# One layer of a hybrid decoder on Trainium2: a sixth place for expert weights, where x lies

## The reference

```python
def _back(x, mods, o_attn, o_conv, gate_a, gate_b, w_pa, w_pb, w_o, g_ffn, ...):
    gate1, shift2, scale2, gate2 = mods
    merged = jax.nn.sigmoid(gate_a) * (o_attn @ w_pa) + jax.nn.sigmoid(gate_b) * (o_conv @ w_pb)
    x = x + gate1 * (merged @ w_o)
    h = _rmsnorm(x, g_ffn) * (1 + scale2) + shift2
    return x + gate2 * _hier_moe(h, w_rg, b_rg, w_re, b_re, w_gate_e, w_up_e, w_down_e)

    # _hier_moe: a row has a weight (combine) for two of the 32 experts, 0 for the others
    a = jnp.einsum('btd,edf->btef', h, w_gate_e)      # w_gate_e, w_up_e: (32, 1024, 256)
    b = jnp.einsum('btd,edf->btef', h, w_up_e)
    return jnp.einsum('btef,efd->btd', jax.nn.silu(a) * b * combine[..., None], w_down_e)  # (32, 256, 1024)
```

## Time and profile before

| | |
|---|---|
| median of 3 runs | 839.25 us (838.13 to 840.46) |
| profiled execution, its own time | 842.34 us |
| its span | 840.6 us |
| TensorE matmuls busy | 711.9 us (85%) |
| VectorE busy | 316.9 us (38%) |
| ScalarE busy | 166.9 us (20%) |
| GpSimd busy | 121.8 us (14%) |
| moved by DMA | 194.72 MB, mean 232 GB/s |
| granted TensorE clock, mean | 0.93 |

### The profile page before, as it was taken

The page is one execution under the profiler, slowest core; times in us unless marked ns, Lnnn a source line. Parts: engine busy times, 40 slices in busy tenths (PEclk is TensorE's granted clock), DMA queues, the critical chain, the costliest instruction groups (busy, mean ns, idle before and its releaser), DMA issues.

```text
span 840.6 us, 12119 instructions
## 1 busy us (share of the span) xinstructions
PE 711.9 (85%) x5001; PEld 543.9 (65%) x5001; DVE 316.9 (38%) x691; ACT 166.9 (20%) x323; POOL 121.8 (14%) x186
## 2 busy tenths in 40 slices
PE   0799999999997799899997999789997888787810
PEld 0389898889997789899993455465554555454500
DVE  0362322136778433323223654435332121212145
ACT  0362222111441432121210111111111010101011
POOL 1500003010040000100000000123333222222011
PEclk9999999999999799999999999769999899999875
DMA  9744466863335036421208910529999999999643
GB/s 296 320 156 172 156 267 234 320 224 111 103 116 175 27 126 275 143 67 51 75 1 309 418 59 25 225 97 379 415 417 414 418 415 419 414 419 415 251 188 154
DMA packets 37439, 194.72 MB, mean 232 GB/s; under 512 B 7106, under 2 KB 7290, under 8 KB 20984
## 3 DMA queue, kind: packets, MB, share of 16 engines
q1 hardware_dynamic: 28512, 171.26, 52.0%
q0 software_dynamic: 8352, 21.81, 7.3%
q10 hardware_dynamic: 520, 0.87, 0.4%
HBM read 186.91 MB, written 15.27 MB: 241 GB/s over the span
## 4 chain that ended last, share of the span: by engine, by line
PE 77%; DVE 8%; DMA 5%; issue 5%; ACT 2%; SPq 1%; POOL 0%; POOLq 0%; DVEq 0%; ACTq 0%
PE bank L1510 29%; PE bank L1744 16%; PE bank L1763 7%; PE bank L1706 6%; PE bank L1654 3%; DMA arena_b<-in_w_ada 3%; PE bank L1449 2%; PE bank L1733 2%; PE bank L1651 2%; PE bank L1546 1%; DMA arena<-in_w_in 1%; PE bank L1671 1%; PE bank L1609 1%; PE bank L1699 1%; ACT arena_b L934 1%
## 5 line engine op out<-in xcount | busy, mean ns | idle before, releaser
L1510 PE MATMUL bank<-h_parts,w_parts 128*128 128x260 f32 x2160 | 276.5, 288 | 1.1 <-DVE w_parts L991 0.9
L1510 PEld LDWEIGHTS bank<-h_parts,w_parts 128*128 128x128 f32 x2160 | 267.1, 192 | 10.1 <-issue 8.7
L1744 PE MATMUL bank<-arena,arena_b 128*64 128x256 f32 x832 | 107.2, 415 | 21.6 <-issue 19.3
L1744 PEld LDWEIGHTS bank<-arena,arena_b 128*64 128x64 f32 x832 | 70.0, 149 | 51.4 <-issue 25.0
L991 DVE TENSOR_TENSOR w_parts<-arena,w_parts 128x1024 fp32r<-128x1024 f32 x46 | 56.3, 1223 | 66.8 <-ACT w_parts L837 66.6
L1340 DVE TENSOR_TENSOR arena_b<-bank,arena_b 128x128 f32<-128x128 f32 x32 | 9.3, 292 | 140.4 <-ACT arena_b L940 140.3
L780 POOL DMA_INDIRECT y_scratch<-arena_b x32 | 33.4, 1044 | 176.5 <-DVE arena_b L1361 161.8
L1706 PE MATMUL bank<-arena,arena_b 128*128 128x512 f32 x128 | 58.6, 612 | 0.0
L837 ACT ACTIVATE w_parts<-arena 128x1024 fp32r<-128x1024 f32 x46 | 48.5, 1054 | 43.2 <-DMA arena<-in_w_in 28.8
L1763 PE MATMUL bank<-arena,arena_b 128*64 128x512 f32 x208 | 49.5, 593 | 0.8 <-DVE arena_b L1346 0.8
L1706 PEld LDWEIGHTS bank<-arena,arena_b 128*128 128x128 f32 x128 | 24.3, 195 | 28.8 <-issue 28.7
(11 more groups left out here) (285 smaller groups left out, 769.8 us busy)
## 6 DMA issues: line engine op xcount, KB each, us to landing
arena<-in_w_gate_up SPq DMA_DIRECT2D x52, 1024.0 KB
arena<-in_w_down SPq DMA_DIRECT2D x26, 1024.0 KB
arena<-in_w_in SPq DMA_DIRECT2D x46, 512.0 KB, 5.1
arena<-in_w_ada SPq DMA_DIRECT2D x22, 1024.0 KB, 7.2
arena_b<-in_w_gate_up SPq DMA_DIRECT2D x12, 1024.0 KB
arena_b<-in_w_down SPq DMA_DIRECT2D x12, 512.0 KB
arena_b<-in_x_prompt SPq DMA_DIRECT2D x8, 512.0 KB, 13.3
arena<-in_w_o SPq DMA_DIRECT2D x2, 2048.0 KB, 8.2
```

What stands on the lines that cost most here:

```text
L1510: ins = pe.matmul(ps[s][:, 0:HALF], w_parts[:, n % 2, wp, k], h_parts[:, hp, k, s * HALF:(s + 1) * HALF], start=(k == 0 and hp == 1), stop ...
L1744: ins = pe.matmul(ps[2 + b][R * hh:R * hh + R, 0:2 * P], hTe[:, b, c * P + jj * R:c * P + jj * R + R], w_gu[slot][jj][:, c, :, hh * P:(hh ...
```

## The change

There is a sixth place. Its gate and up weights are the first 4 x 1024 columns of `X`, half of its down weights the fifth 1024 columns of `X`, and the other half the place of `h2T`. Since x lies there, SP writes each tile of x to a new tensor `x_scratch` in DRAM (`keep_x`) after the tile's two halves are summed: four tiles behind the second issue for expert 4, the last behind expert 3's loads. Expert 5 is loaded into the sixth place when the five writes have landed (`s_xw`), ScalarE has squared all of x (`s_sq2` 10) and the router has read the last of h2T (`s_rt` 5). The loop now starts at expert 6, and an expert e lies in place e mod 6. The last expert in the sixth place is 29; when its down matmuls are done (`s_y` 30) SP reads x back, and VectorE waits for all five tiles (`s_xl`) before it adds the experts' sum. Three semaphores that nothing used are gone; no other instruction of the other engines is added or removed, but the places that their matmuls read change from expert 5 on.

```diff
-SLOTS = 5
+SLOTS = 6
...
         gu_at.append([spare(0, 2 * D), spare(4 * D, 2 * D)])
+        gu_at.append([region("X", 0, 2 * D), region("X", 2 * D, 2 * D)])
...
         dn_at.append([spare(2 * D, D), spare(6 * D, D)])
+        dn_at.append([region("X", 4 * D, D), region("SPLIT", 22 * D, D)])
...
+        x_d = nc.dram_tensor("x_scratch", [T, D], F32).ap()
...
             sp.wait_ge(s_h2, 2)
             load_gate_up(4, 4, 1)
             load_down(4, 4, 1)
+
+            def keep_x(n):
+
+                i = RB[n]
+                sp.wait_ge(s_x2, 2 * n + 2)
+                sp.dma_start(x_d[i * P:i * P + rows[i]], x[0:rows[i], i]).then_inc(s_xw, 16)
+
+            for n in range(4):
+                keep_x(n)
             sp.wait_ge(s_wom, 10)
             for half in range(2):
                 load_gate_up(3, 3, half)
             load_down(3, 3, 0)
+            keep_x(4)
             sp.wait_ge(s_h2, 10)
             load_gate_up(4, 4, 0)
             load_down(4, 4, 0)
+            sp.wait_ge(s_xw, 16 * 5)
+            sp.wait_ge(s_sq2, 10)
+            sp.wait_ge(s_rt, 5)
+            for half in range(2):
+                load_gate_up(5, 5, half)
+                load_down(5, 5, half)
             for e in range(SLOTS, NE):
                 sp.wait_ge(s_gu, e - SLOTS + 1)
...
+            sp.wait_ge(s_y, NE - 2)
+            for i in range(5):
+                sp.dma_start(x[0:rows[i], i], x_d[i * P:i * P + rows[i]]).then_inc(s_xl, 16)
             sp.wait_ge(s_over, 1)
...
+            dve.wait_ge(s_xl, 16 * 5)
             summed(0)
```

More of the change, by code:

```diff
@@ L336, in hybrid_step @@
         s_modT = sem("s_modT")
-        s_modc = sem("s_modc")
         s_mod = sem("s_mod")
@@ L392, in hybrid_step @@
         s_mrg = sem("s_mrg")
-        s_a2 = sem("s_a2")
         s_wom = sem("s_wom")
@@ L415, in hybrid_step @@
         s_over = sem("s_over")
-        s_hz = sem("s_hz")
         s_hg = [sem(f"s_hg{i}") for i in range(EUN)]
@@ L433, in hybrid_step @@
         s_moe = sem("s_moe")
+        s_xw = sem("s_xw")
+        s_xl = sem("s_xl")
         s_yk = [sem(f"s_yk{i}") for i in range(5)]
@@ L441, in hybrid_step @@
         s_pool = sem("s_pool")
-        s_act = sem("s_act")
         plan, batches = [], []
```

## The result

The changed kernel takes 832.94 us (median of 8 runs, 831.22 to 836.03), the kernel before 839.52 in the same comparison (8 runs, 837.34 to 843.20). The ratio is 0.9928, interval 0.9910 to 0.9945: 6.0 us less, between 4.6 and 7.6 (the two medians by themselves are 6.6 us apart). The forecast was 832.5 and 6.8 us less. In a later comparison the same kernel stood at 0.9944 (0.9924 to 0.9965), 4.7 us less. The profiled execution took 835.31 us with a span of 833.4.

A forecast was written before the change was run, and what follows sets the result against it. Weight transfers were taken to set the end between 642 and 793 us. Expert 5's -7.6 plus the gathers' +0.8 gave -6.8 us, 832.5 from the median 839.25; own range 830.5 to 835.5, 8 in 10 for 830 to 837.

The forecast's parts named there:

- Expert 5 out of the stream: Weight stream: 26 experts instead of 27, 3.146 MB at 416 GB/s, 7.6 us gained; bounds 0 and 8.37.
- The late DMA engines: End of the weight stream: gain is that of the slowest engine, 7.8 us, moving the sum by 0.2.
- The writes of x: Before the experts: four hidden in idle DMA time, the fifth delays expert 4's rest 1.3 us; cost 0, uncovered 3.9.
- SP's waits: Before expert 5's load: issue at about 545 us, its load ending near 556.5 and meeting the first gathers.
- The first gathers: Before expert 0's gate-up: delayed beside SP's load, cost 0.8 us, bounds 0 and 5.9.
- The rule of turns packet by packet: First gathers: DMA engines alternate queues by packet, so cost near 0; the forecast kept the trace's 4.1 us to first byte.
- The read-back: End of kernel: x's 2.1 MB in near 794.3 us, before the last scatter; cost 0, uncovered up to 5.1.
- rival 4: GpSimd's queue starves behind SP's at first gather and last scatter, +4.2 us, 843.5; sign: scatter to y load above 3.6; chance 0.05.
- The whole step of 8.4 us: Weight stream: gathers arrive in time and the gain is one whole step, 8.37 us, 830.9; chance 0.10.
- TensorE as the limit: Streaming stretch: TensorE at a lower clock paces the steps, no gain and 0.8 us lost, 840.0; chance 0.05.
- Gathers as late as the h2 write: Start of the experts: first two gathers land 5.9 us late, total 837.5; chance 0.05.
- Starving at both ends: GpSimd's first gather and last scatter each lose 5.9 us behind SP's queue, net +4.2, 843.5; chance 0.05.

The follow-up runs named there:

- the round trip alone: Kernel before, five places, with x written to DRAM and read back as in the change, nothing loaded into its place: 839.32 us, ratio 1.0000.
- the longer load: Kernel before plus x's round trip, an unused load of expert 5, and its two gate-up transfers once more: 845.26 us, ratio 1.0065.
- the unused load: Kernel before plus x's round trip and expert 5's four transfers into x's place, which the experts do not use: 841.33 us, ratio 1.0023.
- late read-back: Changed kernel, but x read back only when all scatters have landed, just ahead of the y loads: 840.71 us, 1.0015 to the kernel before.
- early parts: Changed kernel with half of expert 5's gate-up and down weights loaded sooner, as x's tiles are free: 830.54 and 833.52 us, 0.9909 and 0.9924.
- the run without waiting: Kernel before without the loads of down weights beyond the first five experts: 796.38 us, ratio 0.9490.

## Why the prediction was right

**Expert 5 out of the stream.** Right in mechanism, 0.5 us too large. The eight executions with six places have streams of 221.93 to 222.48 us, mean 222.22; the four with five places have 229.21 to 229.31. That is 7.1 us for an expert, not 7.6; from five places to four it is 7.4. Bytes by rate put a little too much into it. The late DMA engines, by which the estimate drawn from the Trainium skill, "DMA: Bandwidth & Descriptors", section "Latency and other measured facts", came to 7.8, move it the wrong way. What makes the expert cheaper than its bytes was not tried and stays open.

**The writes of x.** Right: the round trip alone costs 0.0 us. They fill the idle stretch, and the fifth is only felt as 0.52 MB in front of expert 5's load.

**SP's waits.** Right: issued at 545.72, about 545 predicted, and SP's queue runs out near 558, predicted 556.5; 0.9 us of both differences is this execution's late start.

**The first gathers.** Right in place, and in size within what the runs can tell. The first bytes come 4.3 us behind the issue (4.1 in the working). The first gate-up is delayed by 8.15 - 6.88 = 1.3 us (1.4 in the second profile), more than the 0.8 of the sum. In the second profile 0.3 of it is the first gather's own instruction, which takes 1.42 us there instead of 1.11. But SP's stream starts only 0.5 and 0.8 us later, since the first gate-up is shorter: 4.76 us against 5.49. In the first profile of each kernel the granted clock is 0.50 (1.2 GHz) until 562 us or shortly behind it (0.99 and 0.82 from 562 to 564), so the later gate-up ran more of its length at the full 2.4 GHz. That the 0.8 fits is thus partly luck: the sum did not have this gain of 0.7 us, and too small a delay made up for it. In the longer load the clock rose later too, and the first gate-up took 5.4 us again. The run with the unused load gives the whole cost as 1.9 us (0.5 to 3.4). The rule of turns packet by packet, in the Trainium skill, "DMA: Bandwidth & Descriptors", section "Queues, rings and completion order", agrees with what the longer load shows once GpSimd's queue has started: 45 of its packets beside 39 of SP's from 558 to 559 us, and since its packets are smaller, 23% of the time. The 3.2 to 4.6 us before the first byte it does not describe.

**The read-back.** Right: hidden, over by 796 us (794.3 predicted), and 6 us where it is not. The sign named for rival 4, more than 3.6 us from scatter to y load, was set too low: the kernel before has 3.64 itself.

**The sum.** In the two profiles of the changed kernel the stream is 6.9 and 7.2 us shorter and the start 0.5 and 0.8 us longer: 6.35 and 6.4 us less, where 6.8 was forecast and 6.0 (4.6 to 7.6) and 4.7 (2.9 to 6.4) were measured. The two spans, 840.6 and 833.4, are 7.2 us apart, since the first profile of the changed kernel started its gathers 0.9 us later and ran its last gate-up in 3.67 us instead of the 5.36 of the earlier trace rows; in the second it took 5.36 again. The range of 830.5 to 835.5 was wider than its reason: a delay of 0 to 3 us gives 831.7 to 834.7.

**The rivals.** The whole step of 8.4 us: out, 7.1. TensorE as the limit: out by the run without later down weights and by the one with four places. Gathers as late as the h2 write: the longer load comes to 7.6 us from issue to landing, so the row of 8.9 is a fair upper bound, but it takes more load than the change has. Starving at both ends: the start half exists in small, the end half does not.

## What to carry to other kernels

Where a stream of weights sets the end, a place more is worth nearly what one place's load takes in the stream (7.1 of 7.6 us here), and it may be paid for with more bytes than it saves if these are moved while the DMA engines are idle: here 4.3 MB went out and back for 3.1 MB of lead. Look at what small, dependent transfers start beside the new load, since they pay for it: count from the queue's end to their issue, and cut the load in parts that go as soon as the tile under each is free (the profiles show 0.6 us for it here, the times do not prove it). And test such a trade by its halves, the traffic without the gain and the gain without the traffic.

## What the runs showed of the hardware

A transfer of GpSimd's queue that was issued while SP's queue was busy had its first bytes 4.1 to 4.6 us after the issue (the h2 write of the earlier trace rows, and the first gather in both profiles of the changed kernel and in those with the late read-back, the unused and the longer load), against 1.75 alone. It was no more with 12 us of load still in SP's queue (the longer load) than with 6; with 4 us, in the run without the round trip, it was 3.2. From then on it had 16% to 33% of the engines while SP's queue stayed full (555 to 561 us in the longer load).

A gate-up of TensorE behind a wait for weights was often, not always, a slow one. In the kernel before ten gate-ups from expert 14 on had a wait of 1.96 us or more before them: nine took 5.1 to 5.4 us, and one, behind 2.28 us, 3.67. The eight behind shorter waits took 3.67. The granted clock in the last, slow one is 0.50 (1.2 GHz) from 795 to 797 us, and 1.00 before it; with early parts a wait of 2.06 us before the last gate-up was followed by 3.67. In the long stretches the mean granted clock is 0.93 and 0.95, while in the run without waiting it stayed at 1.00. So the end of one execution moves by 1.7 us with the clock that the last gate-up happens to meet.
